# A streaming encoder's expert stage: the first two expert tiles of the down projection loaded and split during the last rows of the up projection

## The reference, cut to what matters

```
q      = xt @ peer_w_q                       # 8 heads, two halves of 128
s1, s2 = q[..,0] @ keys1.T, q[..,1] @ keys2.T
best_s, idx = top 16 of the sums of the top 16 of s1 and of s2     # expert = i1 * 128 + i2
gate   = softmax(best_s)
act    = gelu(einsum('thkd,td->thk', peer_u[idx], xt))
out    = einsum('thk,thkd->td', gate * act, peer_v[idx])
h      = layernorm(alpha * h + out)
```

## Time and profile before

| | |
|---|---|
| median of 3 runs | 1517.47 us (1517.31 to 1521.19) |
| the profiled execution, its own time | 1519.15 us |
| its span in the trace | 1517.4 us |
| PE busy | 1401.8 us, 92% of the span, 11201 matmuls |
| DVE busy | 1048.2 us, 69% |
| ACT busy | 686.3 us, 45% |
| POOL busy | 544.9 us, 36% |
| moved by DMA | 168.64 MB, mean 111 GB/s |

### The profile page before, as it was taken

How to read it: one execution, slowest core, us unless ns; L and a number is a source line. 1 busy time by engine, 2 the same in 40 slices (tenths; PEclk the granted TensorE clock), 3 DMA queues, 4 the chain that set the end, 5 groups by cost and what they waited for, 6 DMA issues and landing times.

```text
span 1517.4 us, 34450 instructions
## 1 busy us (share of the span) xinstructions
PE 1401.8 (92%) x11201; PEld 1330.6 (88%) x11201; DVE 1048.2 (69%) x2290; ACT 686.3 (45%) x1450; POOL 544.9 (36%) x675
## 2 busy tenths in 40 slices
PE   6889978875899999999999999998999999999996
PEld 4876767764789898999999999998999999999996
DVE  5334675467659999589999999964555555555555
ACT  3454533222344565744444444444444544444444
POOL 4122242221044999777666676774000000000000
PEclk8998988898989999999999999999999999999999
DMA  3361120000333444444444444444555555555552
GB/s 116 105 182 31 54 70 3 3 3 8 112 98 112 126 138 132 132 125 117 118 115 114 117 117 113 117 130 114 150 149 149 152 146 150 147 151 147 150 149 86
DMA packets 85095, 168.64 MB, mean 111 GB/s; under 512 B 9802, under 2 KB 11346, under 8 KB 84906
## 3 DMA queue, kind: packets, MB, share of 16 engines
q1 hardware_dynamic: 85034, 167.81, 38.8%
HBM read 164.80 MB, written 2.97 MB: 111 GB/s over the span
## 4 chain that ended last, share of the span: by engine, by line
PE 56%; DVE 21%; issue 11%; POOL 5%; ACT 3%; DVEq 2%; DMA 1%; SPq 0%; POOLq 0%; ACTq 0%
PE PS L919 16%; PE PS L920 15%; PE PS L921 15%; DVE W L1365 7%; POOL hlo L552 5%; DVE oh L1759 4%; DVE oh L1758 2%; PE PS L1009 1%; PE PS L907 1%; DVEq L1759 1%; PE PS L1161 1%; DVE AR L1365 1%; PE PS L1171 1%; PE PS L1121 1%; PE PS L1260 1%
## 5 line engine op out<-in xcount | busy, mean ns | idle before, releaser
L552 POOL TENSOR_TENSOR hlo<-hraw,hhiq 128x256 fp32r<-128x256 f32 x512 | 406.9, 804 | 141.6 <-ACT hhiq L593 139.8
L919 PE MATMUL PS<-H1h,hhiq 128*128 128x320 f32 x1024 | 344.4, 336 | 10.2 <-POOL hlo L552 9.0
L593 ACT ACTIVATE hhiq<-hraw 128x256 fp32r<-128x256 f32 x512 | 212.9, 418 | 270.8 <-PE PS L921 240.7
L921 PE MATMUL PS<-Wh,hlo 128*128 128x320 f32 x1024 | 316.9, 310 | 0.0
L921 PE MATMUL PS<-H1h,hlo 128*128 128x320 f32 x1024 | 316.0, 309 | 0.0
L920 PE MATMUL PS<-H1l,hhiq 128*128 128x320 f32 x1024 | 315.0, 308 | 0.0
L919 PEld LDWEIGHTS PS<-H1h,hhiq 128*128 128x128 f32 x1024 | 193.6, 189 | 13.9 <-POOL hlo L552 9.0
L920 PEld LDWEIGHTS PS<-H1l,hhiq 128*128 128x128 f32 x1024 | 193.6, 189 | 0.0
L921 PEld LDWEIGHTS PS<-Wh,hlo 128*128 128x128 f32 x1024 | 192.8, 188 | 0.0
L921 PEld LDWEIGHTS PS<-H1h,hlo 128*128 128x128 f32 x1024 | 192.2, 188 | 0.0
L1365 DVE TENSOR_TENSOR W<-PS,W 128x320 f32 (+3 forms) x168 | 150.7, 897 | 24.5 <-ACT PS L593 22.8
(11 more groups left out here) (319 smaller groups left out, 2656.9 us busy)
## 6 DMA issues: line engine op xcount, KB each, us to landing
hraw<-in_uT SPq DMA_DIRECT2D x256, 256.0 KB, 2.6
hraw<-in_vE SPq DMA_DIRECT2D x256, 256.0 KB, 2.6
wraw<-in_wbig SPq DMA_DIRECT2D x50, 512.0 KB, 3.6
xin<-in_xT SPq DMA_DIRECT2D x4, 336.0 KB, 3.8
out_yT<-XF SPq DMA_DIRECT2D x4, 320.0 KB
ckx<-in_ckT SPq DMA_DIRECT2D x1, 1024.0 KB, 8.5
vs<-in_cv SPq DMA_DIRECT2D x1, 768.0 KB, 10.2
out_ko<-kx SPq DMA_DIRECT2D x1, 672.0 KB
```

Of the source, the lines that this page charges most:

```text
L552: nc.gpsimd.tensor_tensor(hlo[q // 2 % 4][:, cols_], hraw[q // 2 % 4][:, cols_], hhiq[q % 4][:].bitcast(F32), ALU.subtract).then_inc(s_hlo ...
L593: return nc.scalar.activation(out, in_, f, **kw)
L919: mm(out, whi_, xhi, start=start, stop=False)
L921: return mm(out, wlo_, xhi, start=False, stop=stop)
```

## The change

Expert 0's two half tiles get their own place, `vraw0` and `vlo0` over it, in the half of `oh` that hhv[0] and hhv[1] do not use. SP loads them once the last one-hot matmul is through (`s_grid` 80), between up loads 243 and 244; for that the last three passes of SP's loop are written out. ACT makes Wh of row 0 and hhv[0] behind the GELU of row 123, hhv[1] behind that of row 124 and Wh of row 1 behind that of row 125; its last four rows are written out for that. DVE makes Wl[0] and vlo0[0] behind the W product of row 124, vlo0[1] behind that of row 125 and Wl[1] behind that of row 126. PE's first down reads vlo0. Expert 1's half tiles stay where they were: loaded into hraw[2] and hraw[3] at s_up_mm 510 and 512, cast and subtracted after the last row.

```diff
--- before.py
+++ after.py
@@ -186,6 +186,8 @@
         unit = tail.put("unit", [P, 1])
         hhv = [at(f"hhv{i}", [P, 512], hole_at + 2048 * i, F32R) for i in range(2)] + hhi
         oh = at("oh", [P, OH_SLOTS, 2, NK], hole_at)
+        vraw0 = [at(f"vraw0{i}", [P, 512], hole_at + 4096 + 2048 * i) for i in range(2)]
+        vlo0 = [at(f"vlo0{i}", [P, 512], hole_at + 4096 + 2048 * i, F32R) for i in range(2)]
         assert hole_at + OH_SLOTS * 2 * NK * 4 <= TAIL
         wsplit = Region(pairs_at, SBUF_END)
         Wh = [wsplit.put(f"Wh{i}", [P, TQ], F32R) for i in range(2)]
@@ -439,11 +441,19 @@
             sp.wait_ge(s_mxl, NJ + NG)
             for q in range(4):
                 sp.dma_start(hraw[q][:], uT[q]).then_inc(s_hraw[q], 16)
-            with sp.Fori(1, 2 * NI // 4) as k:
+            last = (E0 + NGR + 2) // 2
+            with sp.Fori(1, last) as k:
                 for q in range(4):
                     sp.wait_ge(s_up_mm, k * 8 + (2 * q - 6))
                     sp.dma_start(hraw[q][:], uT[bass.ds(k * 4 + q, 1)].rearrange("a p c -> (a p) c")).then_inc(s_hraw[q], 16)
-            for q in range(4):
+            sp.wait_ge(s_grid, NGR)
+            for q in range(2):
+                sp.dma_start(vraw0[q][:], vE[q]).then_inc(s_vraw[q], 16)
+            for k in range(last, 2 * NI // 4):
+                for q in range(4):
+                    sp.wait_ge(s_up_mm, k * 8 + 2 * q - 6)
+                    sp.dma_start(hraw[q][:], uT[k * 4 + q]).then_inc(s_hraw[q], 16)
+            for q in range(2, 4):
                 sp.wait_ge(s_up_mm, 4 * NI - 6 + 2 * q)
                 sp.dma_start(hraw[q][:], vE[q]).then_inc(s_vraw[q], 16)
             with sp.Fori(1, 2 * NI // 4) as k:
@@ -867,26 +877,39 @@
             with act.Fori(GATED, GRID0) as k:
                 up_rest(k)
             up_rest(GRID0, direct=(True, False, False, False))
-            with act.Fori(GRID0 + 1, NI // RIT) as k:
+            with act.Fori(GRID0 + 1, NI // RIT - 1) as k:
                 up_rest(k, direct=(False,) * RIT)
+
+            def down_w(e, s):
+                A(Wh[s][:], W[:, bass.ds(e, 1), :].rearrange("p a t -> p (a t)"), ACT.Copy).then_inc(s_wh, 1)
+
+            def down_v(b, s, load, src):
+                act.wait_ge(s_vraw[2 * s + b], load)
+                A(hhv[2 * s + b][:], src, ACT.Copy).then_inc(s_vhi, 1)
+
+            def down(e, s, load):
+                act.wait_ge(s_down, e * 2 - 2)
+                down_w(e, s)
+                for b in range(2):
+                    act.wait_ge(s_down, e * 2 + (b - 3))
+                    down_v(b, s, load, hraw[2 * s + b][:])
+
+            for e in range(NI - RIT, NI):
+                for x in range(4):
+                    quarter(4 * e + x, (4 * e + x) % 16, 16 * (e // 2 + 1))
+                gelu(e - 1, e - 1, False)
+                if e == NI - RIT:
+                    act.wait_ge(s_w, NGR)
+                    down_w(0, 0)
+                    down_v(0, 0, 16, vraw0[0][:])
+                if e == NI - RIT + 1:
+                    down_v(1, 0, 16, vraw0[1][:])
+                if e == NI - RIT + 2:
+                    down_w(1, 1)
             gelu(NI - 1, NI - 1, False)
-
-
-            def down(e, s, load):
-                if not isinstance(e, int) or e >= 2:
-                    act.wait_ge(s_down, e * 2 - 2)
-                A(Wh[s][:], W[:, bass.ds(e, 1), :].rearrange("p a t -> p (a t)"), ACT.Copy).then_inc(s_wh, 1)
-                for b in range(2):
-                    act.wait_ge(s_vraw[2 * s + b], load)
-                    if not isinstance(e, int):
-                        act.wait_ge(s_down, e * 2 + (b - 3))
-                    A(hhv[2 * s + b][:], hraw[2 * s + b][:], ACT.Copy).then_inc(s_vhi, 1)
-
-            act.wait_ge(s_w, NGR)
-            for e in range(2):
-                if e:
-                    act.wait_ge(s_up_mm, 4 * NI)
-                down(e, e, 16)
+            act.wait_ge(s_up_mm, 4 * NI)
+            for b in range(2):
+                down_v(b, 1, 16, hraw[2 + b][:])
             act.wait_ge(s_gm, NI - E0)
             with act.Fori(1, NI // 2) as k:
                 for e in range(2):
@@ -1331,7 +1354,8 @@
                     for kk in range(4):
                         if start and b == 0:
                             pe.wait_ge(s_gm, NI - E0 - 3 + kk)
-                        ins = three(PS[:, 4 * b + kk, 0:TQ], hhv[2 * s + b][:, P * kk:P * kk + P], hlo[2 * s + b][:, P * kk:P * kk + P],
+                        lo_ = vlo0[b] if start else hlo[2 * s + b]
+                        ins = three(PS[:, 4 * b + kk, 0:TQ], hhv[2 * s + b][:, P * kk:P * kk + P], lo_[:, P * kk:P * kk + P],
                                     Wh[s][:], Wl[s][:], start, stop)
                     ins.then_inc(s_down, 1)
 
@@ -1809,20 +1833,31 @@
                     step_of(k * RIT + j, j)
             for i in range(NGR - RIT, NGR + 1):
                 step_of(i, i)
-            for r in range(NGR - 1, NI - E0):
-                gelu_row(r, r, NGR)
-
-
-            def down(e, s):
+            def down_w(e, s):
                 dve.wait_ge(s_wh, e + 1)
                 tt(Wl[s][:], W[:, bass.ds(e, 1), :].rearrange("p a t -> p (a t)"), Wh[s][:].bitcast(F32),
                    ALU.subtract).then_inc(s_wl, 1)
+
+            def down_v(e, b, s, dst, src):
+                dve.wait_ge(s_vhi, e * 2 + (b + 1))
+                tt(dst[:], src[:], hhv[2 * s + b][:].bitcast(F32), ALU.subtract).then_inc(s_vlo, 1)
+
+            def down(e, s):
+                down_w(e, s)
                 for b in range(2):
-                    dve.wait_ge(s_vhi, e * 2 + (b + 1))
-                    tt(hlo[2 * s + b][:], hraw[2 * s + b][:], hhv[2 * s + b][:].bitcast(F32), ALU.subtract).then_inc(s_vlo, 1)
-
-            for e in range(2):
-                down(e, e)
+                    down_v(e, b, s, hlo[2 * s + b], hraw[2 * s + b])
+
+            for r in range(NGR - 1, NI - E0):
+                gelu_row(r, r, NGR)
+                if r == NI - E0 - 4:
+                    down_w(0, 0)
+                    down_v(0, 0, 0, vlo0[0], vraw0[0])
+                if r == NI - E0 - 3:
+                    down_v(0, 1, 0, vlo0[1], vraw0[1])
+                if r == NI - E0 - 2:
+                    down_w(1, 1)
+            for b in range(2):
+                down_v(1, b, 1, hlo[2 + b], hraw[2 + b])
             with dve.Fori(1, NI // 2) as k:
                 for e in range(2):
                     down(k * 2 + e, e)
```

## The result

The changed kernel took 1512.43 us (median of 18 runs, 1508.6 to 1519.0), the kernel before 1518.87 us (18 runs, 1511.81 to 1526.93): a ratio of 0.9962, 95% interval [0.9947, 0.9976], or 5.8 us less (3.6 to 8.0). The ratio is the record's estimate from the single runs and not the quotient of the two medians, which differ by 6.4 us. Single runs of either kernel differ by 10 us and more, so the whole time says only that it is faster, by 0.24 to 0.53% in one set and by 0.02 to 0.30% in the other. What the change does is read from the trace, where the seam can be measured to 0.1 us.

A forecast was written before the change was run, and what follows sets the result against it. TensorE was taken as the bound, busy throughout down, leaving only the seam between up and down. Gain 5.41 - 0 (feed) - 1.3 (clock) = 4.1 us, from the median 1517.47 to 1513.4 us; range 1509.5 to 1516.6.

The forecast's parts named there:

- Halves 0 and 1 start at once: Start of down: expert 0's halves start right after the last up matmul, at 1037.73, and are through at 1041.25.
- Half 2 waits for hlo behind H1s: Expert 1's first half: DVE's hlo ends 0.56 us after POOL's H1s; PE stalls 3.1 us; gain there 5.41 us.
- a fixed delay: Seam, alternative to waiting for H1s: first such DVE operation is delayed 4.6 us; hlo[2] ends 0.6 us later; no chance given.
- Nothing for half 4 and later: Down after expert 1: Wl behind the two hlos is done 1.3 us ahead of half 4's slot at 1047.9.
- The DMA queue: Late up: two early loads make uT load 244 0.7 us late against 0.75 us slack; cost 0, bounds 0 and 1.3.
- ACT, DVE, POOL in rows 124 to 127: Last up rows: moved casts and subtractions cost 0; up to 0.3 us on ACT, 0 to 0.4 us through POOL.
- The clock falls: Around the gap before expert 1: half clock for 3.4 us costs 1.3 us, bounds 1.1 and 1.5.
- my first case: Seam: DVE held up behind H1s and the clock falls; gain 4.1 us, 1513.4 us; chance 0.56.
- the clock holds: Rival, seam: same path but no clock fall; gain 5.4 us, 1512.1 us; chance 0.25.
- DVE was held up: Judges the rival that DVE is not held up in the seam: gain 8.5 us, 1509.0 us; chance 0.07.
- The feed did not starve: Judges the rival that the last up rows' feed starves: costs 2.0 us, gain 2.1, 1515.4 us; chance 0.08.
- DVE's and ACT's loops show no pause: Judges the rival that a down loop fetches code every pass: 42 us slower, 1556 us; chance 0.04.

The follow-up runs named there:

- e1: Changed kernel with POOL's H1s addition cut into eight parts, one behind every eighth half of down, instead of one block in the seam; ratio 0.9944 to the kernel before.
- e2: Kernel before, without the change's early tile, with H1s in eight parts instead of one block; ratio 0.9961 to the kernel before.
- e4: Changed kernel with H1s in one block but started behind half 60 of down instead of in the seam; ratio 0.9968 to the kernel before.
- a0: The changed kernel run once more with no edit, beside the kernel before; ratio 0.9984, median 1514.95 us.
- e5: Changed kernel's early loads and tiles alone; ACT and DVE cast and subtract both experts in the seam as before; ratio 1.0012 to the kernel before.
- e8: The early loads alone, ACT and DVE splitting both experts in the seam, with H1s in eight parts; ratio 0.9971 to the kernel before.
- e6: Changed kernel with four early loads in the queue instead of two; ratio 0.9986 to the kernel before.
- e9: Same kernel as e1, run again for a narrower interval; ratio 0.9942 to the kernel before.

## Why the prediction was right, point by point

The forecast was 1513.4 us, 4.1 us less, by one named path. The measured times are 1512.43 us and a gain of 5.8 us (3.6 to 8.0); the seam of the profiled execution says 3.8. That the median came within 1 us of the forecast is partly luck: the kernel before had 1517.47 us as the median of three runs and 1518.87 of 18, so the forecast started 1.4 us lower, and the gain by medians was 6.4 us. The path is what was right.

- *Halves 0 and 1 start at once.* Right: 0.00 and 1.76 us. Strip 3's wait for row 127, which I dropped at 0.06, does not show.
- *Half 2 waits for hlo behind H1s.* Right, and the central step. hlo[2] was to start 1.7 us after up and started 1.72 (1040.07 - 1038.35); PE was to stand for 3.1 us and stood for 3.07 (2.92 by the trace's own idle time). hlo was to end 0.56 us after H1s and ended 0.57. The gain at half 2 was put at 5.41 and is 12.04 - 6.60 = 5.44. That the cause is H1s, and not a late tile or a fixed delay, the profile of before only suggested; e1, e2 and e4 show it.
- *Nothing for half 4 and later.* Right: from half 2 on the distances differ by the clock alone.
- *The DMA queue, 0 with a lateness of 0.7 us.* Right in this profile, by a margin of 0.1 us. From the last grid matmul to the end of up it is 28.38 us in both kernels (1037.73 - 1009.35 and 1038.35 - 1009.97). The last grid matmul of the kernel before, in its timeline:

```profile
1009.35 0.38 PE L1293 MATMUL PS<-oh 128*128 128x128 f32 x2
```

  and that of the changed kernel, with ACT's next late cast:

```profile
1009.97 0.38 PE L1316 MATMUL PS<-oh 128*128 128x128 f32 x2
...
1015.67 0.73 ACT L603 ACTIVATE hhiq<-hraw 128x256 fp32r<-128x256 f32 x2 [1.02 <-PE PS L944]
```

  The cast of quarter 488 starts 5.70 us behind that grid matmul; before, it was 1014.46 - 1009.35 = 5.11. So the cast was 0.6 us late and the slack took it. The trace names PE as the releaser of this cast, but the PE step that it needs (s_up_mm 485) was through near 1038.35 - 27 x 0.88 = 1014.6, a microsecond earlier; what came last must have been the load. In a0 the trace names it:

```profile
1013.70 0.72 ACT L603 ACTIVATE hhiq<-hraw 128x256 fp32r<-128x256 f32 x2 [1.23 <-DMA hraw<-in_uT]
```

  There the cast was 0.8 us late and PE lost 0.1. The slack was 0.69 us (5.80 - 5.11), near the 0.75 of the sum, but the lateness with two loads was 0.6 to 1.1 us in eight profiles, not 0.7: the term was 0 in two of them, 0.1 in four, 0.26 in e5 and 0.45 in e8, within the bounds of 0 and 1.3. With two loads more (e6) it was 1.2 us.
- *ACT, DVE, POOL in rows 124 to 127: 0.* Right: no PE wait in up after the grid stage. What was paid is seen in POOL's groups (1011 to 1036 us), where hlo took 739 ns on average before:

```profile
L562 POOL TENSOR_TENSOR hlo<-hraw,hhiq 128x256 fp32r<-128x256 f32 x29 | 21.9, 773 | 4.1 <-ACT hhiq L603 3.5
```

  and in one DVE vlo of 0.86 us instead of 0.69. By the lengths each held the other for a while, within the slack.
- *The clock falls, 1.3 us.* Right in kind, too small in size: 1.5 to 1.6 us, at or above its upper bound of 1.5 (half 2 to half 8 takes 12.17 us, 10.56 at full clock, and 10.63 behind the same gap in e6, where the clock held). This term is why the seam gained 3.8 us and not 4.1. But the step that led there, that a gap of 3.1 us falls because it is nearest to one of 3.29 us that did, was weak. The same gap of 2.92 us had a fall in two profiles (after, a0) and none in a third (e6); one of 2.33 us had a fall in e2 and none in e8. So both my first case and the rival "the clock holds" occur, each in single executions of seams with the same gap, worth 3.8 and 5.4 us at half 8. The kernels are not quite the same (e6 has two loads more and a PE wait 28 us earlier, e8 has the early loads and e2 has not), and no kernel was profiled both ways. What decides stays open; no run here separates it.

The rivals: DVE was held up, so 8.5 us was not to be had by this change (it is what e1 gets). The feed did not starve: it cost 0 to 0.1 us in the changed kernel. DVE's and ACT's loops show no pause: PE is busy for all 434.00 us, so the code that moved costs nothing. The chances were 0.45 for faster by over 0.3% and 0.50 for within; the measured ratio, 0.38% less in one set of runs and 0.16% in the other, lies on both sides of that line.

## What to carry to other kernels

When work is moved out of a seam, ask which instruction of another engine held it up there, and whether that one stays: here it did, and the stall moved from expert 0 to expert 1 and kept 3 of its 7 us. A long POOL instruction with SBUF inputs that is itself off the critical path can hold a DVE operation with two SBUF inputs to its own end, 4 us here. Cut into eight pieces, each of which ended before DVE's next such operation, it cost nothing. And price a gap of PE with its clock: 1.5 to 1.6 us more than its length here where the clock fell.

## What the runs showed that was not expected

POOL waits for DVE too. The eight parts of H1s were recorded at 1.33 us each, not at 5.6 / 8 = 0.7 us:

```profile
L592 POOL TENSOR_TENSOR H1s<-H1h,H1l x8: 1294/1330/1366, 1051.7 to 1150.3; 128x320 f32<-128x320 f32 x8
```

The first part of e1, with the DVE hlo around it:

```profile
1051.56 0.69 DVE L1392 TENSOR_TENSOR hlo<-hraw,hhi 128x512 fp32r<-128x512 f32 x1 [0.47 <-ACT hhi L606]
1051.69 1.29 POOL L592 TENSOR_TENSOR H1s<-H1h,H1l 128x320 f32<-128x320 f32 x1 [12.07 <-PE PS L947]
```

It started 0.13 us into the hlo and ended 0.73 us behind the hlo's end. So did all 32 parts of e1, e2, e8 and e9: they started 0.00 to 0.29 us into an hlo and ended 0.73 to 0.75 us behind it, as if the part began only when the hlo was through. Each part was released at the end of a half of down, where DVE begins an hlo, so DVE was not held, which is why they cost PE nothing; parts that start just ahead of an hlo were not tried. The other surprise is the clock: behind gaps that agree to 0.01 us, in kernels that differ only in small edits, it fell or held, so a single profile can be off by a term of 1.5 us in either direction.
